# The local group's rotary halves laid 64 rows apart, swapped by two ScalarE copies; its k kept per kv head over 128 rows; another step order

## The chip, the cores and the metric

One core of a Trainium2 chip runs the kernel. The metric is the device time of one execution in microseconds (us); it is the median of three runs. The engines are TensorE (PE; its weight loads are PEld), VectorE (DVE), ScalarE (ACT), GpSimd (POOL) and SyncE (SP, which issues DMAs).

## The reference

Two layers over 512 tokens of width 1024, all in float32. Each layer normalises, projects, runs two attention groups, projects back, and runs an MLP:

```python
for l in range(DEPTH):                                   # DEPTH = 2
    h = rmsnorm(x, attn_norm[l])
    proj = jnp.einsum('bsd,de->bse', h, w_in[l])         # 2304 columns
    sb_q, sb_k, sb_v, sw_q, sw_k, sw_v = jnp.split(proj, splits, axis=-1)
    sb_o = stick_breaking_attention(sb_q, sb_k, sb_v)    # 8 heads of 64, causal, no softmax
    sw_q = rope(sw_q, positions)                         # 8 query heads of 64
    sw_k = rope(sw_k, positions)                         # 2 kv heads of 64
    sw_o = sliding_window_sink_attention(sw_q, sw_k, sw_v, sinks[l])   # window 128
    mix = concatenate([rmsnorm(sb_o, sb_norm[l]), rmsnorm(sw_o, swa_norm[l])])
    x = x + mix @ w_out[l]
    h = rmsnorm(x, mlp_norm[l])
    x = x + square(relu(h @ w_up[l])) @ w_down[l]        # 4096 wide
# rope: out = [x1 * cos - x2 * sin, x2 * cos + x1 * sin], x1 and x2 the two halves (32 each) of a head
```

## The kernel before

Activations are kept transposed: rows are features, 512 columns are tokens. Each float32 operand of the large products is split into a high part (rounded to fp32r) and a low part (the rest), and a product is three matmuls: high by high, high by low, low by high (L405 to L407). For the weights ACT makes the high part (step CH, L604) and POOL the low part (step CL, L804), and SP loads the next pack after it (L366).

The input projection makes 18 tiles of 128 rows. Tile n is made by the steps T (first four chunks of the contraction, 12 matmuls) and U (last four, 12 more) in bank n mod 2 of the PSUM tensor D. So tile n + 2 can start only when tile n is out of its bank. The way out depends on the kind of tile:

- q and k of the stick-breaking group: TE (DVE multiplies by the norm's factor, L989), TH (ACT writes the high part, L679 or L682), TL (DVE writes the low part, L1004 or L1008; then the bank counts as drained, L1011). For k of this group TH and TL are two instructions each, one for each head, with the other head's rows set to zero by a column of head_rows.
- v tiles: TE into kf, VT (PE transposes), VH and VL (ACT and DVE split).
- q and k of the local group (swq 0 to 3 and swk, the rotary tiles): RE (ACT copies the tile to kf, L689; SP then issues four DMAs of 32 rows that lay the halves exchanged into the one tensor turned, L381), RM (POOL multiplies turned by sin_r, L854), RS (DVE multiplies the tile in its bank by cos_r, L993), RA (DVE adds the two, L998), TH, TL. sin_r and cos_r have the norm's factor in them and are made once in each layer by the step RR (L973, L975). The next RE waits until the RA before it is done with turned.

The rotary tiles are tiles 3, 4, 5, 9 and 10 of the first layer and 1, 2, 3, 9 and 10 of the second. Tile 5 of the first layer and tile 2 of the second are k.

The local attention works in 8 steps n (two groups of heads by four blocks of 128 queries): WS (PE: 4 matmuls that lay the band mask, L482, and 12 of scores, L487, over 64 rows, as the two kv heads lie in rows 0 to 63 and 64 to 127), WM, WE, WR, WN (softmax), WT (PE transposes), WH, WL, WA (PE: probabilities by v, L511), WO, WD, SQ and SA (squares for the norm). The stick-breaking attention works head by head: BS (PE scores, L525, L527), BE (ACT: three functions, L703 to L707), BP (DVE, L1021), BH (ACT, L710), BL (DVE, L1025), BX (PE: suffix sums, L537), XE and XH (ACT, L714, L719), XL (POOL, L849), BA (PE, L550), BO, BD. BS of the next head waits for XE of the one before, as all heads share the PSUM tensor Z.

The norm's factor of the input (rms_a) comes from PE sums of squares (steps NP and NA, L417) and a chain NAD, NAE, NAF on DVE and ACT. AG0 to AG11 (DVE) make the rotary angles and SN (ACT, with two table loads) their sine and cosine; both belong to the first layer. OS is the output projection of the local part, OE adds it to x.

The order of all steps is one written list for each layer (ORDER_0, ORDER_1). Every engine walks the list and takes the steps that are its own, in the order of the list; semaphores do the rest. After the lists come the output projection of the stick-breaking part and the MLP, as loops.

## Time and profile before

| | |
|---|---|
| median of three runs | 1242.49 us (1240.52 to 1242.96) |
| the profiled execution, its own time | 1243.44 us |
| its span, first to last instruction | 1241.6 us |
| mean granted TensorE clock | 0.982 of full |
| busy: PE, DVE, ACT, POOL | 95%, 43%, 44%, 46% of the span |

The profile's times count from the first instruction of the span. The first layer's attention stage, with its two projections, runs from 11 us to about 268 us, its MLP to 623 us, the second layer's attention stage from there to about 870 us. The share of busy time is a mean over all stages; "idle before" tells how long an engine stood before an instruction, and the name behind the arrow what it waited for.

### The profile page before, as it was taken

How to read it: one execution, taken by the hardware profiler on the slowest of the kernel's cores; microseconds unless marked ns; L12 is line 12 of the kernel's file. 1: busy time of each engine (PE TensorE's matmuls, PEld its weight loads, DVE VectorE, ACT ScalarE, POOL GpSimd, SP SyncE). 2: the span in 40 equal slices, each digit the busy share in tenths (PEclk: the TensorE clock that was granted, in tenths of full speed). 3: DMA queues.
4: the chain of work that ended last, by engine and by line, in shares of the span. 5: the costliest groups of instructions: out<-in, count | busy, mean ns of one | idle time of the engine just before them, and what ended most of it. 6: DMA issues, size and time to landing. Idle time of an engine off the chain costs nothing.

```text
span 1241.6 us, 15277 instructions
## 1 busy us (share of the span) xinstructions
...
## 2 busy tenths in 40 slices
...
GB/s 179 77 86 51 45 42 35 68 48 105 114 90 102 102 84 101 101 84 101 85 85 77 60 68 48 48 25 60 102 102 102 88 105 96 93 105 89 100 69 68
DMA packets 30773, 102.20 MB, mean 82 GB/s; under 512 B 4224, under 2 KB 4224, under 8 KB 30720
## 3 DMA queue, kind: packets, MB, share of 16 engines
...
## 4 chain that ended last, share of the span: by engine, by line
PE 84%; DVE 6%; ACT 4%; issue 2%; POOL 1%; DMA 1%; DVEq 1%; ACTq 0%; SPq 0%; POOLq 0%
PE D L405 24%; PE D L407 24%; PE D L406 24%; PE Z L537 4%; PE Z L525 2%; PE O L550 1%; PE W L487 1%; DVE xm L910 1%; PE O L511 1%; PE W L497 1%; PE W L482 1%; PE W L417 1%; DMA x<-in_x 1%; DVE stage L1025 1%; POOL turned L854 1%
## 5 line engine op out<-in xcount | busy, mean ns | idle before, releaser
L804 POOL TENSOR_TENSOR w<-raw,w 128x1024 fp32r<-128x1024 f32 x178 | 432.7, 2433 | 412.7 <-ACT w L604 404.1
L604 ACT ACTIVATE w<-raw 128x1024 fp32r<-128x1024 f32 x177 | 186.0, 1052 | 212.1 <-PE D L407 201.0
L405 PE MATMUL D<-stage,w 128*128 128x512 f32 x576 | 225.4, 391 | 0.0
L407 PE MATMUL D<-stage,w 128*128 128x512 f32 x576 | 224.2, 389 | 0.0
L406 PE MATMUL D<-stage,w 128*128 128x512 f32 x576 | 224.1, 389 | 0.0
L405 PE MATMUL D<-xm,w 128*128 128x512 f32 x512 | 200.7, 392 | 5.1 <-POOL w L804 2.7
L406 PE MATMUL D<-xm,w 128*128 128x512 f32 x512 | 199.3, 389 | 0.0
L407 PE MATMUL D<-xm,w 128*128 128x512 f32 x512 | 199.2, 389 | 0.0
L405 PE MATMUL D<-xa,w 128*128 128x512 f32 x352 | 143.7, 408 | 23.1 <-DVE xa L910 11.3
L1108 DVE TENSOR_TENSOR kf<-o 128x512 f32<-128x512 f32 x64 | 64.3, 1004 | 189.4 <-ACT o L774 189.3
L1122 DVE TENSOR_TENSOR D<-D,probs 128x512 f32<-128x512 f32 x64 | 44.8, 699 | 229.4 <-PE D L407 229.4
L407 PE MATMUL D<-xa,w 128*128 128x512 f32 x352 | 139.5, 396 | 0.0
L406 PE MATMUL D<-xa,w 128*128 128x512 f32 x352 | 139.4, 396 | 0.0
L405 PEld LDWEIGHTS D<-stage,w 128*128 128x128 f32 x576 | 108.3, 188 | 22.7 <-issue 0.5
L406 PEld LDWEIGHTS D<-stage,w 128*128 128x128 f32 x576 | 108.3, 188 | 22.6 <-issue 0.5
L407 PEld LDWEIGHTS D<-stage,w 128*128 128x128 f32 x576 | 108.1, 188 | 22.6
L405 PEld LDWEIGHTS D<-xm,w 128*128 128x128 f32 x512 | 96.1, 188 | 27.8 <-DVE xm L910 4.1
L406 PEld LDWEIGHTS D<-xm,w 128*128 128x128 f32 x512 | 96.1, 188 | 20.1 <-issue 0.5
L407 PEld LDWEIGHTS D<-xm,w 128*128 128x128 f32 x512 | 96.1, 188 | 20.1
L405 PEld LDWEIGHTS D<-xa,w 128*128 128x128 f32 x352 | 67.4, 191 | 40.2 <-issue 14.9
L774 ACT ACTIVATE o<-D 128x512 f32<-128x512 f32 x64 | 38.1, 595 | 136.9 <-PE D L407 136.9
L407 PEld LDWEIGHTS D<-xa,w 128*128 128x128 f32 x352 | 67.4, 191 | 14.8
...
## 6 DMA issues: line engine op xcount, KB each, us to landing
...
inv_freq<-in_inv_freq SPq DMA_DIRECT2D x1, 0.5 KB, 4.5
sinks<-in_sinks SPq DMA_DIRECT2D x1, 8.0 KB, 7.0
```

The costliest lines, as they stand in the source:

```text
L405: pe.matmul(bank, w[:, slot, 0, k], rhs[:, 0, c], start=start, stop=False)
L406: pe.matmul(bank, w[:, slot, 0, k], rhs[:, 1, c], start=False, stop=False)
L407: mm = pe.matmul(bank, w[:, slot, 1, k], rhs[:, 0, c], start=False, stop=stop)
L417: return pe.matmul(W[:, 0, :], minus_one[:, :].bitcast(F32), squares, start=start, stop=stop)
L482: pe.matmul(dst[g], ident_r[:, :], band[:, at0:], start=True, stop=False)
L525: pe.matmul(dst, k[:, kl, j * P:(j + 1) * P], q[:, ql, j * P:T], start=f == 0 and j != 3, stop=False, skip_group_check=True)
L537: mm = pe.matmul(Z[:, at0:Z_AT[j] + Z_LEN[j]], (minus_tri if jj == j else minus_one)[:, :], sp[:, f, Z_AT[jj]:Z_AT[jj] + Z_LEN[jj]], start ...
L604: act.activation(w[:, slot_of(at_layer), 0], raw[:, p % 2], ACT.Identity).then_inc(w_hi, 1)
L774: act.activation(relu[c % 2], D[:, (MLP_TILE + c) % 2], ACT.Relu).then_inc(mlp_relu, 1)
L804: pool.tensor_tensor(w[:, slot, 1], raw[:, p % 2], w[:, slot, 0].bitcast(F32), ALU.subtract).then_inc(w_ready, 1)
L1108: dve.tensor_tensor(kf[:, c % 2], relu[c % 2], relu[c % 2], ALU.mult).then_inc(mlp_sq, 1)
L1122: dve.tensor_tensor(D[:, tile % 2], D[:, tile % 2], rms2, ALU.mult)
```

## The change

The columns of w_in for the local group's q and k are permuted on the host, so that a rotary tile has the first halves of its two heads in rows 0 to 63 and the second halves in rows 64 to 127; the frequencies of rows 0 to 63 are negative. A rotary tile now goes out of its bank so: TE (DVE, the norm's factor, in place), RE (two ACT copies of 64 rows each, to the other half of kf), RM (POOL: kf by sin, in place), RS (DVE: the bank by cos), RA (DVE: adds kf), TH, TL. The four DMAs, the tensor turned, sin_r, cos_r and the step RR are gone, and RE no longer waits for the RA of the rotary tile before. A row half now holds rows of both kv heads, so k is kept once for each kv head over all 128 rows with the other head's rows zero (group_rows): its TH and TL are two instructions each, and the 12 score matmuls of WS go over 128 rows. Squares of the local output (SQ) go to rms_w. Both step lists are new. Cut to its core:

```diff
@@ -107,40 +107,40 @@
 
 
 ORDER_0 = """
-AG0 T0 NP0 CH3 NA0 AG1 NAD0 U0 NAE0 NAF0 TE0 CL3 AG2 TH0 T1 TL0 U1 CH4 CL4 AG3 AG4 T2 TE1 CH5 TH1 TL1 CL5 U2
-T3 AG5 TE2 VT2 VH2 CH6 AG6 AG7 AG8 AG9 AG10 VL2 U3 RE3 AG11 CL6 RM3 T4 U4 SN0 RR0 BS0 CH7 RS3 RA3 RE4 TH3 TL3
-RS4 RM4 BE0 T5 RA4 TH4 CH8 U5 BP0 TL4 T6 RE5 BH0 RM5 U6 BL0 RS5 RA5 CL7 TE6 TH5 TL5 VT6 WS0 VH6 VL6 WM0 WE0
...
-BH4 WD5 BL4 CL17 WT6 TE15 BO3 TE14 BX4 WH6 SQ5 WL6 SA4 WS7 BD3 VT15 XE4 TH14 WM7 TL14 WA6 CH18 VH15 CL18 WO6
-WE7 BS5 VL15 WR7 T16 XH4 U16 WD6 BE5 WN7 WT7 T17 BP5 XL4 WH7 SA5 WL7 BH5 BL5 WA7 U17 BX5 CH19 TE16 TH16 WO7
-SQ6 WD7 TL16 SQ7 CL19 SA6 CH20 SA7 NW0 NWD0 XE5 NWE0 NWF0 TE17 MN0 BS6 VT17 BE6 CL20 CH21 MN1 GH0 BP6 MN2 BH6
...
-OS1 OE0 XL6 BO5 BP7 BH7 BD5 CH22 GH2 BL7 OS2 BA6 OE1 BX7 BO6 CL21 GL2 XE7 OE2 OS3 OE3 XH7 CL22 OS4 CH23 BD6
-OE4 XL7 BA7 BO7 OS5 BD7 OE5 OS6 CH24 NS0 CL23 CL24 GH3 NSD0 NSE0 GL3 OS7 OE6 NSF0 OE7
+T0 U0 NP0 CH3 AG0 AG1 NA0 AG2 NAD0 NAE0 T1 U1 NAF0 TE0 TH0 AG3 TL0 AG4 T2 TE1 U2 CH4 AG5 CL3 TH1 TL1 T3 TE2
+VT2 AG6 VH2 AG7 AG8 AG9 AG10 U3 CH5 VL2 AG11 SN0 TE3 RE3 CL4 CH6 T4 U4 RS3 RM3 CL5 RA3 TH3 TE4 TL3 BS0 RE4 T5
+RM4 RS4 RA4 TH4 U5 CL6 BE0 TL4 TE5 BP0 RE5 BH0 T6 RS5 RM5 BL0 CH7 RA5 U6 TH5 BX0 CH8 CL7 TE6 TL5 VT6 XE0 WS0
+WM0 WE0 WR0 CL8 VH6 XH0 VL6 BS1 CH9 T7 WN0 WT0 WH0 WL0 XL0 T8 WS1 BE1 CL9 CH10 WM1 WE1 BP1 WA0 U7 WO0 WR1 WN1
+TE7 U8 WT1 TH7 CL10 WH1 WD0 BH1 TL7 WL1 TE8 SQ0 T9 TH8 WS2 CH11 U9 BL1 WA1 WM2 SA0 TE9 WE2 WO1 WR2 BX1 RE9 XE1
+WN2 BA0 WD1 RM9 BO0 WT2 RS9 TL8 WH2 BS2 CH12 RA9 WL2 WS3 WM3 BD0 BE2 T10 WA2 CL11 CH13 TH9 CL12 BP2 WE3 U10
...
+SQ4 WD5 BH4 BL4 U15 BA3 WN6 WT6 TH14 WH6 BX4 XE4 TE15 VT15 BO3 WL6 TL14 WS7 VH15 SA3 WM7 SQ5 BS5 T16 WA6 VL15
+XH4 U16 WE7 BD3 BE5 WR7 SA4 WN7 WO6 BP5 WT7 CH18 T17 TE16 WH7 WD6 WL7 BH5 WA7 XL4 CL18 SA5 CH19 SQ6 BL5 WO7
+U17 WD7 SA6 SQ7 TH16 GH0 BX5 SA7 NW0 XE5 GL0 TL16 NWD0 NWE0 NWF0 GH1 BS6 BE6 MN0 CL19 GL1 TE17 VT17 VH17 BP6
+MN1 BH6 BA4 MN2 BL6 XH5 BO4 MH0 BD4 MH1 BX6 MH2 XE6 MN3 ML0 XL5 BA5 MH3 BS7 BO5 ML1 XH6 BE7 ML2 XL6 CH20 ML3
+CL20 OS0 VL17 BD5 BP7 OS1 BH7 OE0 BA6 GH2 OE1 CH21 BO6 OS2 BL7 CH22 BX7 OS3 CL21 XE7 XH7 BD6 OE2 CH23 CL22 OE3
...
 """
 ORDER_1 = """
-T0 CH3 NA0 T1 U0 NAD0 NAE0 CL3 U1 NAF0 RR0 TE0 TH0 RE1 TL0 RS1 CH4 CH5 RM1 T2 RA1 U2 TH1 TL1 RE2 CL4 RS2 T3 U3
-RM2 RA2 RE3 TH2 TL2 RS3 RM3 RA3 CH6 CL5 T4 TH3 CL6 TL3 U4 WS0 TE4 T5 WM0 WE0 VT4 VH4 CH7 U5 VL4 TE5 WR0 TH5
-WN0 T6 TL5 WT0 WH0 CH8 BS0 U6 WL0 BE0 CL7 BP0 WS1 T7 BH0 TE6 WM1 BL0 U7 CH9 VT6 WE1 WR1 BX0 TE7 VH6 XE0 VL6
...
+T0 CH3 NA0 NAD0 CL3 U0 T1 NAE0 NAF0 TE0 TH0 TL0 U1 T2 TE1 CH4 RE1 RS1 U2 RM1 CH5 RA1 CL4 TH1 TL1 TE2 RE2 RM2
+RS2 CL5 RA2 T3 TH2 TL2 CH6 U3 TE3 CL6 RE3 T4 U4 RS3 CH7 RM3 RA3 TH3 TL3 TE4 WS0 WM0 WE0 T5 VT4 VH4 WR0 U5 WN0
+CL7 VL4 WT0 T6 WH0 TE5 TH5 U6 TL5 TE6 BS0 WL0 WS1 CH8 VT6 CL8 T7 U7 BE0 WM1 CH9 VH6 BP0 VL6 CL9 BH0 BL0 WE1
+TE7 WR1 TH7 CH10 T8 BX0 WA0 WN1 WT1 XE0 WH1 WL1 WO0 BS1 WS2 TL7 U8 BE1 WD0 WM2 WA1 BP1 WE2 WR2 SQ0 BH1 T9 CH11
...
 """
...
         w = sb("w", [P, SPLIT_SLOTS, 2, KC, P], F32R)
         work = sb("work", [P, 2, Z_ALL])
-        ksw = sb("ksw", [P, 2, T], F32R)
+        ksw = sb("ksw", [P, KV_HEADS, 2, T], F32R)
         qsw = sb("qsw", [P, 2, 2, T], F32R)
         vsw = sb("vsw", [P, NB, KV_HEADS, 2 * DH], F32R)
         probs = sb("probs", [P, 4, 2 * P])
@@ -262,9 +262,8 @@
...
         kf = sb("kf", [P, 2, T])
-        turned = sb("turned", [P, T])
         head_rows = sb("head_rows", [P, 2])
-        sin_r = sb("sin_r", [P, T])
+        group_rows = sb("group_rows", [P, KV_HEADS])
...
         count, turns, theta = Z3[:, 0, :], cos[:, :], sin[:, :]
-        cos_r = rms_w[:, :]
-        sq_w = turned[:, :].rearrange("p (s i t) -> p s i t", s=2, i=2)
+        sq_w = rms_w[:, :].rearrange("p (s i t) -> p s i t", s=2, i=2)
...
-                    elif step == "RE":
-                        r = plan.re_use[step, n]
-                        sp_.wait_ge(kf_moved, l * ROPE_TILES + r + 1)
-                        for a in range(4):
-                            b = a ^ 1
-                            sp_.dma_start(turned[b * 32:b * 32 + 32, :], kf[a * 32:a * 32 + 32, n % 2]
-                                          ).then_inc(turned_in, 16)
...
-                                    half = slice(g * DH, (g + 1) * DH)
-                                    mm = pe.matmul(dst[g], qsw[half, i, ql, b * P:(b + 1) * P],
-                                                   ksw[half, kl, k0 * P:(b + 1) * P], start=False, stop=f == 2)
+                                    mm = pe.matmul(dst[g], qsw[:, i, ql, b * P:(b + 1) * P],
+                                                   ksw[:, g, kl, k0 * P:(b + 1) * P], start=False, stop=f == 2)
...
+                        elif kind == "swk":
+                            for g in range(KV_HEADS):
+                                last = act.activation(ksw[:, g, 0], D[:, n % 2], ACT.Identity, scale=group_rows[:, g:g + 1])
...
                     elif step == "RE":
-                        act.wait_ge(tile_done, l * DENSE + n + 1 + CREDIT)
-                        if plan.re_use[step, n]:
-                            before = next(x for x in plan.re_use if plan.re_use[x] == plan.re_use[step, n] - 1)[1]
-                            act.wait_ge(scaled, l * IN_TILES + plan.scaled["RA", before] + 1)
-                        act.activation(kf[:, n % 2], D[:, n % 2], ACT.Identity,
-                                       scale=SCALE if plan.tiles[n][0] == "swq" else 1.0).then_inc(kf_moved, 1)
+                        act.wait_ge(scaled, l * SCALES + plan.scaled["TE", n] + 1)
+                        for a in range(2):
+                            last = act.activation(kf[head(1 - a), n % 2], D[head(a), n % 2], ACT.Identity)
+                        last.then_inc(kf_moved, 1)
...
                     elif step == "SQ":
                         pair, b = divmod(n, NB)
                         act.wait_ge(swa_o, l * SWA_STEPS + n + 1)
-                        act.wait_ge(scaled, l * IN_TILES + plan.scaled["RA", plan.rope_last] + 1)
...
                     elif step == "RM":
-                        pool.wait_ge(turned_in, (l * ROPE_TILES + plan.re_use["RE", n] + 1) * 64)
-                        pool.wait_ge(sin_ready, l + 1)
-                        pool.tensor_tensor(turned[:, :], turned[:, :], sin_r[:, :], ALU.mult).then_inc(turned_sin, 1)
+                        pool.wait_ge(kf_moved, l * ROPE_TILES + plan.re_use["RE", n] + 1)
+                        pool.wait_ge(trig, 1)
+                        pool.tensor_tensor(kf[:, n % 2], kf[:, n % 2], sin[:, :], ALU.mult).then_inc(turned_sin, 1)
...
-                    elif step == "RR":
-                        dve.wait_ge(trig, 1)
-                        dve.scalar_tensor_tensor(sin_r[:, :], sin[:, :], -1.0, rms_a[:, :], ALU.mult, ALU.mult
-                                                 ).then_inc(sin_ready, 1)
-                        dve.tensor_tensor(cos_r, cos[:, :], rms_a[:, :], ALU.mult)
-                        dve.drain()
...
@@ -986,16 +979,16 @@
                         kind, j = plan.tiles[n]
                         dst = kf[:, n % 2] if kind in ("sbv", "swv") else D[:, n % 2]
                         dve.wait_ge(tile_done, l * DENSE + n + 1 + CREDIT)
-                        dve.scalar_tensor_tensor(dst, D[:, n % 2], SCALE if kind == "sbq" else 1.0, rms_a[:, :],
+                        dve.scalar_tensor_tensor(dst, D[:, n % 2], SCALE if kind in ("sbq", "swq") else 1.0, rms_a[:, :],
                                                  ALU.mult, ALU.mult).then_inc(scaled, 1)
                     elif step == "RS":
                         dve.wait_ge(kf_moved, l * ROPE_TILES + plan.re_use["RE", n] + 1)
-                        dve.scalar_tensor_tensor(D[:, n % 2], D[:, n % 2], SCALE if plan.tiles[n][0] == "swq" else 1.0, cos_r,
-                                                 ALU.mult, ALU.mult)
+                        dve.wait_ge(trig, 1)
+                        dve.tensor_tensor(D[:, n % 2], D[:, n % 2], cos[:, :], ALU.mult)
                         dve.drain()
                     elif step == "RA":
                         dve.wait_ge(turned_sin, l * ROPE_TILES + plan.re_use["RE", n] + 1)
-                        dve.tensor_tensor(D[:, n % 2], D[:, n % 2], turned[:, :], ALU.add).then_inc(scaled, 1)
+                        dve.tensor_tensor(D[:, n % 2], D[:, n % 2], kf[:, n % 2], ALU.add).then_inc(scaled, 1)
...
+                        elif kind == "swk":
+                            for g in range(KV_HEADS):
+                                last = dve.scalar_tensor_tensor(
+                                    ksw[:, g, 1], D[:, n % 2], group_rows[:, g:g + 1],
+                                    ksw[:, g, 0].bitcast(F32), ALU.mult, ALU.subtract)
...
-    in_columns[3 * SB_W:3 * SB_W + SWA_W] = 3 * SB_W + swa_rows
+    turn = np.arange(P).reshape(2, 2, DH // 2).transpose(1, 0, 2).reshape(-1)
+    in_columns[3 * SB_W:3 * SB_W + SWA_W] = 3 * SB_W + swa_rows.reshape(PAIRS, P)[:, turn].reshape(-1)
+    in_columns[3 * SB_W + SWA_W:3 * SB_W + SWA_W + P] = 3 * SB_W + SWA_W + turn
...
-    inv_freq[(np.arange(P) // half) % 2 == 1] *= -1
+    inv_freq[:DH] *= -1
...
```

## Rows read from the trace of the kernel before

**Rows 1.** Windows: stretch, then PE, PEld, DVE, ACT, POOL busy, clock, DMA

```profile
291.00:626.00 335.00, 335.00 (x1477) 277.12 (x1477) 103.20 (x136) 107.89 (x139) 156.55 (x68) 1.00 0.29 96
...
671.10:792.00 120.90, 120.45 (x716) 103.38 (x716) 64.98 (x100) 91.33 (x157) 62.18 (x34) 1.00 0.18 57
```

**Rows 2.** Waits of PE in 641:653 us, then in 50:66 us (sum, times, longest)

```profile
PE D L405 <- DVEq L1011: 4.9, 2, 2.6
...
PE D L405 <- DVEq L1011: 2.1, 2, 1.0
PE D L468 <- DVE kf L989: 0.8, 1, 0.8
```

**Rows 3.** Timeline, the rotary chain of tile 1, second layer (start, us, instruction)

```profile
636.38 0.60 ACT L689 ACTIVATE kf<-D 128x512 f32<-128x512 f32 x1 [1.11 <-PE D L407]
...
637.00 9.92 SPq L381 DMA_DIRECT2D turned<-kf  x8
...
640.87 1.29 POOL L854 TENSOR_TENSOR turned<-turned,sin_r 128x512 f32<-128x512 f32 x1 [10.92 <-DMA turned<-kf]
...
642.19 0.70 DVE L998 TENSOR_TENSOR D<-D,turned 128x512 f32<-128x512 f32 x1 [4.48 <-POOL turned L854]
```

**Rows 4.** Timeline of PE: where tiles and BX7 start late, and what follows

```profile
175.75 0.54 PE L405 MATMUL D<-xa,w 128*128 128x512 f32 x1 [1.87 <-DVEq L1011]
...
180.17 0.39 PE L405 MATMUL D<-xa,w 128*128 128x512 f32 x1
...
226.05 0.73 PE L537 MATMUL Z<-stage,minus_tri 128*128 128x512 f32 x2 [2.15 <-DVE stage L1025]
...
644.44 0.47 PE L405 MATMUL D<-xa,w 128*128 128x512 f32 x1 [2.56 <-DVEq L1011]
...
652.50 0.47 PE L405 MATMUL D<-xa,w 128*128 128x512 f32 x1 [2.34 <-DVEq L1011]
...
656.60 0.63 PE L405 MATMUL D<-xa,w 128*128 128x512 f32 x1
```

**Rows 5.** Groups of instructions by form (busy us, mean ns, idle before)

```profile
L989 DVE SCALAR_TENSOR_TENSOR D<-D,rms_a 128x512 f32<-128x512 f32 x16 | 11.1, 697 | 4.8 <-PE D L407 3.9
...
L724 ACT ACTIVATE other<-O 64x512 f32<-64x512 f32 x16 | 9.5, 593 | 11.8 <-PE O L550 11.6
...
L1025 DVE TENSOR_TENSOR stage<-work,stage 128x1280 fp32r<-128x1280 f32 x16 | 26.6, 1660 | 7.7 <-ACT stage L710 7.3 <-issue 0.2
```

**Rows 6.** Timeline of PE: a whole step WS1, and a step WA1

```profile
76.16 0.45 PE L482 MATMUL W<-band,ident_r 128*128 128x256 f32 x2
...
78.07 0.50 PE L405 MATMUL D<-xa,w 128*128 128x512 f32 x1
...
94.94 1.12 PE L511 MATMUL O<-pt,vsw 128*128 128x256 f32 x8
95.89 0.70 PE L537 MATMUL Z<-stage,minus_tri 128*128 128x512 f32 x2
```

**Rows 7.** Timeline of PE, first layer: NP0 begins, its wait, U0, T2

```profile
16.14 1.02 PE L417 MATMUL W<-acc,minus_one 128*128 128x512 f32 x2
...
18.84 1.13 PE L417 MATMUL W<-probs,minus_one 128*128 128x512 f32 x2 [1.68 <-DVE probs L943]
...
21.97 0.80 PE L405 MATMUL D<-xa,w 128*128 128x512 f32 x1
...
31.28 0.47 PE L405 MATMUL D<-xa,w 128*128 128x512 f32 x1 [0.56 <-DVEq L1011]
```

**Rows 8.** Timeline of DVE and POOL, first layer: before TL14, and around BL7

```profile
171.63 2.37 DVE L1055 SCALAR_TENSOR_TENSOR small<-small,neg_sink 128x4 f32<-128x4 f32 x1
...
174.16 1.40 DVE L1004 SCALAR_TENSOR_TENSOR xm<-D,head_rows,xm 128x512 fp32r<-128x512 f32 x2
...
222.41 3.58 DVE L1025 TENSOR_TENSOR stage<-work,stage 128x1280 fp32r<-128x1280 f32 x1 [0.21 <-issue]
...
222.27 2.38 POOL L804 TENSOR_TENSOR w<-raw,w 128x1024 fp32r<-128x1024 f32 x1 [3.08 <-ACT w L604]
```

More of the change, by code:

```diff
@@ L115 @@
-WR2 WN2 WD1 TL8 XH1 WT2 BO0 WH2 RS9 BD0 RM9 BS2 WL2 RA9 T10 WS3 U10 XL1 BE2 TH9 CH13 WM3 TL9 WE3 WA2 RE10 T11
-CL13 BP2 BA1 WR3 WN3 WT3 WO2 RM10 BH2 BO1 CH14 WH3 RS10 WD2 BL2 WL3 RA10 TH10 BD1 U11 SQ0 BX2 TL10 TE11 SA0
-WA3 T12 XE2 WS4 WO3 SQ1 WM4 SQ2 XH2 CH15 TH11 TL11 WE4 WR4 U12 BS3 WN4 WT4 WD3 BE3 TE12 WH4 SA1 XL2 BP3 T13
-VT12 WL4 U13 WS5 VH12 VL12 TE13 SQ3 WM5 WA4 BH3 BL3 TH13 CL14 TL13 WE5 T14 BX3 WO4 WR5 XE3 CH16 BA2 WN5 WT5
-BS4 CL15 WH5 XH3 BO2 WD4 T15 SA2 BE4 SQ4 CL16 WL5 WS6 WM6 BD2 CH17 WE6 BP4 U14 WA5 WO5 WR6 XL3 U15 BA3 SA3 WN6
@@ new lines @@
+XE3 TH13 WD4 U14 CH17 BO2 XH3 TL13 WH5 SA2 BS4 CL16 BE4 BD2 WL5 XL3 WS6 WM6 WA5 T15 WE6 TE14 BP4 WR6 CL17 WO5
+SQ4 WD5 BH4 BL4 U15 BA3 WN6 WT6 TH14 WH6 BX4 XE4 TE15 VT15 BO3 WL6 TL14 WS7 VH15 SA3 WM7 SQ5 BS5 T16 WA6 VL15
+XH4 U16 WE7 BD3 BE5 WR7 SA4 WN7 WO6 BP5 WT7 CH18 T17 TE16 WH7 WD6 WL7 BH5 WA7 XL4 CL18 SA5 CH19 SQ6 BL5 WO7
+U17 WD7 SA6 SQ7 TH16 GH0 BX5 SA7 NW0 XE5 GL0 TL16 NWD0 NWE0 NWF0 GH1 BS6 BE6 MN0 CL19 GL1 TE17 VT17 VH17 BP6
+MN1 BH6 BA4 MN2 BL6 XH5 BO4 MH0 BD4 MH1 BX6 MH2 XE6 MN3 ML0 XL5 BA5 MH3 BS7 BO5 ML1 XH6 BE7 ML2 XL6 CH20 ML3
```

54 lines of the change are left out of this document (30 added, 24 removed).

## The prediction

> **What bounds the kernel.** I read the windows first. In the MLP PE is busy 335.00 of 335 us, and from 671 to 792 us, the middle of the second layer's attention, 120.45 of 120.9 [rows 1]. So PE's own work sets the time, and another engine's work is worth something only where PE stands. I then read PE's waits by stretch and its timeline for the places. Those that touch this change are few. Ahead of T3 and T4 of the second layer PE stands 4.9 us, ahead of T5 and T6 of the first 2.1 us [rows 2], each time for a bank that a rotary tile leaves late. Elsewhere it stands 1.68 us inside NP0 [rows 7], 1.87 us ahead of T16 and 2.15 us ahead of BX7 in the first layer [rows 4]. After some of these the granted clock falls to its half level: T16 takes 180.17 - 175.75 = 4.42 us and T4 656.60 - 652.50 = 4.10 us [rows 4], where such a block takes some 2.8 (12 matmuls, 0.23 us apart).
>
> **The second layer's start.** Before, tile 1's chain is: copied at 636.38, four DMAs, POOL at 640.87, DVE's add at 642.19 [rows 3], then TH and TL, and T3 at 644.44 [rows 4]: 8.1 us. From the copy's end (636.98) to POOL's start are 3.9 us of DMA. The new chain is TE 0.70, two copies of 64 rows (0.59 each, L724, together 1.1 to 1.2), POOL 1.29, add 0.70, TH 0.60 (as the copy that it resembles), TL 0.70 (as the add) [rows 3, 5], and some 0.3 of hand-overs: 5.4 us. RS lies beside POOL's multiply as before. So bank 1 is free at 641.8, and PE, which came to it at 644.44 - 2.56 = 641.9, doesn't wait: 2.5 us gained. The wait that RE has for the add before it is gone, but it would not have been the last one.
>
> Tile 2 is k. It is done when T3 starts, 641.9. Its chain is 5.4 us, a second TH and TL (0.60 and 0.70) and a hand-over: 6.8, so T4 can start at 648.7. PE gets there at 641.9 + 5.7 = 647.6, waits 1.1, and is 652.50 - 648.7 = 3.8 ahead. Its longest idle stretch there is now 1.1 in place of 2.56 and 2.34, so I take the half-clock stretch in T4 (4.10 - 2.8 = 1.3) as gone: 5.1 us in all; I take 5.0. Tile 3 is done at 647.6; its TE waits behind TL2 until 648.7, and 5.4 later, at 654.1, it is out; WS0 comes at 648.7 + 5.7 = 654.4 and does not wait. RM1 and RM3 stand behind CL steps in POOL's queue, but those wait for splits that ACT makes earlier than now. Bounds: 3.7 if the clock still falls, 5.5 if T4 waits only 0.7.
>
> **The first layer's start.** U0 now stands ahead of NP0. PE fills the 1.68 us wait, but the sums start at 16.14 + 2.73 = 18.87, where the second of them could go on at 18.84 before [rows 7]; the first is now behind it (0.86), so the norm's factor comes 0.8 later. T2 waits for tile 0, and that for the factor: 31.28 + 0.8 = 32.1, with PE standing 3.8 us ahead of it rather than 0.56, as U0 and U1 are done by 28.3. That is a loss of 0.8, and 1.3 more if the clock falls there as it did in T16. Behind it the waits of T5 and T6, 2.1 us, and of VT6, 0.8 [rows 2], go: the same 2.7 us come off each rotary chain. SN0 now stands ahead of RE3, so tile 3's chain starts only after the tables (0.7 to 1.3 us past the old RE3's end) and takes back much of that for T5. BX0 and WS0 wait some 0.7 as BX0 is moved ahead of WS0. Sum: 2.1 + 0.8 - 0.8 - 0.7 = 1.4 without a fall of the clock, 0.1 with it. I take 0.8.
>
> **T16.** In DVE's list TL14 stood behind WM7 and BD3. WM7's 128x4 instruction took 2.37 us, TL14 came at 174.16 [rows 8], and PE stood 1.87 and then ran at half clock (4.42 - 2.8 = 1.6) [rows 4]. TL14 now stands ahead of WM7 and BD3, and TH14 ahead of XE4, so bank 0 is free before BS5 ends. The next gates, BX5 and NW0, hang on the same engines, which follow PE. Gain 3.2, between 1.9 (no clock) and 3.5.
>
> **BX7.** BL7 took 3.58 us, against 1.66 in its group [rows 5, 8]: it began 0.14 after a POOL split that took 2.38, and ended 1.3 after it. In the new list CH20 stands right behind BE7, so this split falls some 3 us earlier and reaches only the first 0.6 us of BL7. BL7 then ends near 223.4, when PE is still at BA6. The wait of 2.15 [rows 4] goes; I leave the clock behind it. Gain 2.1, between 0 (another split on the same spot) and 3.7 (with the clock).
>
> **Scores over 128 rows.** A step WS has 16 matmuls before and after. Before, it takes 78.07 - 76.16 = 1.91 us. WA has 8 matmuls of 256 columns over 128 rows, each with its own weight load, and takes 95.89 - 94.94 = 0.95, so 0.119 each [rows 6]. 16 x 0.119 = 1.90. So the wider rows cost nothing there, and I put 0.3 us for the four steps of 128 columns. Upper end: at 1.12 / 8 = 0.14 each the step takes 2.24, and 16 steps cost 5.3; lower end 0.
>
> A rule speaks against this edit. The Trainium skill, "TensorE: Matmul & The Clock Gate", Part 3 (Packing small matmuls), says that matmuls of few rows in distinct row groups run concurrently, starting within about 4 ns of each other. By it the 12 products now run as 6 pairs, the old step costs 10 slots, and the sum would be that of the rival below. The trace doesn't bear out a step of 10 slots.
>
> **The added work in the queues.** ACT gets 10 second copies and 2 second TH (7.1 us), DVE 10 TE and 2 second TL less 4 instructions of RR (about 5.6). POOL's work is the same, SP loses 40 DMAs and issues weights no later. The tiles of the two starts are in the chains above. In the middle are four tiles (9 and 10, twice). ACT has 29.6 us free of 120.9 there, DVE 56 [rows 1]; the rotary tiles have 10 us and more of PE work between U and the tile that wants their bank. If that cover is gone, the four cost 0.70 + 0.59 each, 5.2 us. New waits from a list in another order fall here too. I take 0.9.
>
> **The sum.** 5.0 + 0.8 + 3.2 + 2.1 - 0.3 - 0.9 = 9.9 us. The profiled execution took 1243.44 us for a span of 1241.6; it would take 1233.5, the span 1231.7. The median lies 0.95 below the profiled one's: 1242.5 - 9.9 = 1232.6.
>
> **Rivals.**
> *Given back in the tails.* The end of each layer's stage is a chain of heads through ACT and DVE. If T16 and BX7 only move their waits to BX6, 5.3 go: 1237.9. For it: BX7's gain hangs on half a microsecond between POOL and DVE. Against: T16's wait ends at a DVE queue, which is reordered. Chance 0.15.
> *Nothing stays.* The second layer's gain is also met by later waits: about 1242. Against it, PE stands 0.45 us in 120.9 behind it [rows 1]. Chance 0.06.
> *The pairs are lost.* If the score products pair up fully now, a WS step loses 6 slots of 0.119, 0.71 us, times 16: 11.4 in place of 0.3, and the time is 1243.7. Against it stands that the step takes 1.91 us and not 10 slots, 1.19 [rows 6]. Chance 0.04.
> *Slower: the heads fall behind.* ACT's list is filled up where a head's chain (BE, BH, XE) has to be ready when PE comes to BX. Each such miss costs its wait and then a half-clock block, as at T16: 1.87 + 1.6 = 3.5 us [rows 4]. Three such misses eat the gain; from 12.4 us, so with four among the heads that PE doesn't wait for now, the kernel is slower by over 0.2%: 1232.6 + 14 = 1246.6. For it: less PE work lies between BS4 and BX4 of the first layer than before (U14 has moved ahead of BS4). Against: ACT's 29.6 us of room. Chance 0.10.
>
> **How the numbers follow.** My forecast has 0.65. The range: best case 5.5 + 1.4 + 3.5 + 3.7 = 14.1 with nothing lost, so 1228.4, and other meetings of DVE and POOL can give a microsecond more: 1227. Its upper end takes in the rival in the tails and half of the unknown bounds: 1239.5. Left out are the last three rivals, 0.20. 0.2% is 2.5 us, about what a measurement can tell from no change. Faster by more than that (forecast and first rival): 0.80. Within: 0.10. Slower: 0.10.
>
> **What would show it.** T3 of the second layer without a wait and T4 with about 1.1; no half clock there; T2 of the first layer with a wait near 3.8; T16 right behind BS5; a WS step of about 1.9 us; BL7 near 2 us. I would be wrong if WS took 2.3 or more, if PE showed waits of over 1 us between 90 and 170 or in the second layer's middle, or if T2 started a long half-clock stretch.

## The result, and the profile after

The changed kernel takes 1223.74 us (1223.23 to 1226.46, 4 runs) against 1242.14 (1240.52 to 1242.96, 4 runs) for the kernel before: ratio 0.9858, 95% interval 0.984 to 0.9876. It is 18.4 us faster; 9.9 were forecast, and the time lies 3.3 us below the forecast range. The profiled execution of the changed kernel is the slowest of its four, 1226.46 us, span 1224.6, so the two traces differ by 17.0 us. The medians differ by 1.4 more. One execution of each kernel was profiled, so what the granted clock happened to do in that one is in every difference of the two traces.

PE does 5574 matmuls in both. So the time can be located by a *lead*: how much earlier than in the kernel before PE begins the same step, after the same PE work. The lead is 1.0 at tile 9 of the first layer, 4.6 behind T16, 8.0 behind BX7, 10.4 at the second layer's first matmul, 16.3 when its starting tiles are done, and 17.7 at the end of its list and at PE's last matmul. Over the whole span it is 17.0: the last 0.7 go in the output's stores, behind PE's work.

**The second layer's start.** PE's waits in 636 to 650 us, the stretch that answers to [rows 2]:

```profile
PE D L400 <- DVEq L1009: 1.2, 1, 1.2
```

The timeline of tile 1's chain, from TE to TL, with T3 on PE below it. It answers to [rows 3] and to T3 in [rows 4]; columns as there:

```profile
625.94 0.70 DVE L982 SCALAR_TENSOR_TENSOR D<-D,rms_a 128x512 f32<-128x512 f32 x1 [1.76 <-PE D L402]
...
627.95 1.29 POOL L853 TENSOR_TENSOR kf<-kf,sin 128x512 f32<-128x512 f32 x1 [8.43 <-ACT kf L684]
...
629.27 0.70 DVE L991 TENSOR_TENSOR D<-D,kf 128x512 f32<-128x512 f32 x1 [0.67 <-POOL kf L853]
630.63 0.69 DVE L1006 TENSOR_TENSOR qsw<-D,qsw 128x512 fp32r<-128x512 f32 x1 [0.66 <-ACT qsw L679]
...
631.52 0.47 PE L400 MATMUL D<-xa,w 128*128 128x512 f32 x1 [0.18 <-DVEq L1009]
```

The chain takes 631.32 - 625.94 = 5.4 us, and 5.6 to the start of T3, where it was 8.1. Tile 2, with its second TH and TL, goes from TE at 631.46 to the end of TL at 636.83 + 1.41 = 638.24: 6.8 us.

**The tail of the first layer.** Windows of the changed kernel around T2, T16, BX7 and the second layer's first tiles (columns as in [rows 1]):

```profile
31.53:35.55 4.02, 4.02 (x13) 3.18 (x13) 2.93 (x4) 0.60 (x1) 1.77 (x1) 0.68 0.31 89
171.72:175.00 3.28, 3.28 (x18) 2.60 (x18) 2.62 (x6) 3.21 (x11) 0.01 (x1) 1.00 0.00 0
219.65:222.50 2.85, 2.85 (x22) 2.75 (x21) 1.36 (x2) 1.06 (x1) 2.21 (x2) 1.00 0.30 108
631.50:644.00 12.50, 11.26 (x49) 8.95 (x50) 6.25 (x9) 6.25 (x9) 7.43 (x5) 1.00 0.36 126
```

and of the kernel before around T16, BX7 and T4 of the second layer, the blocks of [rows 4]:

```profile
175.75:180.17 4.42, 4.42 (x12) 3.50 (x13) 1.71 (x5) 4.22 (x7) 3.15 (x2) 0.61 0.22 84
226.05:230.50 4.45, 4.45 (x21) 4.36 (x22) 2.02 (x3) 0.00 (x0) 0.00 (x0) 0.63 0.28 107
652.50:656.60 4.10, 4.10 (x13) 3.19 (x14) 0.90 (x2) 0.03 (x1) 1.57 (x2) 0.67 0.21 51
```

The third number from the end is the granted clock. T16, BX7 and T4 each stood behind a wait of 1.9 to 2.3 us and ran mostly at the lower level (1.2 GHz); in the changed kernel T16 and BX7 wait for nothing, T4 waits 1.22, and all three run at the full 2.4 GHz. T2 of the first layer has the one new block at the lower level, behind a wait of 2.58 us.

Not each of these blocks comes whenever its wait does. The traces of the experiments below have the same waits again. BX7's of 2.1 us has a block at the lower level behind it in all five traces that have it. T16's of 1.9 us has one in two of six (before and `x_wide_scores`). `x_ch22` has the wait, 1.89 us, and then:

```profile
175.85:178.80 2.95, 2.95 (x13) 2.45 (x14) 1.71 (x5) 2.87 (x5) 1.68 (x1) 1.00 0.32 126
```

So 1.6 us of what the trace of before shows at T16 come in some executions and not in others. T2's wait of 2.58 us has a block at the lower level behind it in two of five traces (the changed kernel and `y_t16`).

**A place that was not forecast.** DVE and POOL of the kernel before, just past the end of the first layer's list, where NSF0 makes the norm's factor for the MLP in three operations (the timeline):

```profile
247.00 0.69 DVE L902 TENSOR_TENSOR rms_a<-rms_a,work 128x512 f32<-128x512 f32 x1
248.14 2.86 DVE L904 SCALAR_TENSOR_TENSOR rms_a<-rms_a,work 128x512 f32<-128x512 f32 x1 [0.44 <-issue]
...
248.08 2.37 POOL L804 TENSOR_TENSOR w<-raw,w 128x1024 fp32r<-128x1024 f32 x1 [3.95 <-ACT w L604]
...
251.91 0.47 PE L405 MATMUL D<-xa,w 128*128 128x512 f32 x1 [2.35 <-DVE x L1090]
```

(the last row is PE, at the second tile behind the list) and of the changed kernel:

```profile
239.79 0.69 DVE L903 SCALAR_TENSOR_TENSOR rms_a<-rms_a,work 128x512 f32<-128x512 f32 x1
...
240.12 2.63 POOL L798 TENSOR_TENSOR w<-raw,w 128x1024 fp32r<-128x1024 f32 x1 [3.96 <-ACT w L598]
```

Before, the third operation pauses 0.44 us, comes 0.06 after POOL's low part and takes 2.86; after, there is no pause, it comes 0.33 ahead of POOL and takes 0.69. OE7 stands behind NSF0 in DVE's order, and PE waits 2.35 us for OE7's bank before and not at all after. The lead rises by 2.45 there.

### The profile page after: what moved, and what is told of

Its sections match the earlier page's. It is cut to its first block, busy times and chain, and to the rows that moved or that the text cites. A ratio compares the mean times of both kernels' runs of the same rounds, so it can differ in the third digit from the quotient of the medians.

```text
span 1224.6 us, 15260 instructions
## 1 busy us (share of the span) xinstructions
PE 1173.8 (96%) x5574; PEld 980.7 (80%) x5574; DVE 543.0 (44%) x719; ACT 555.8 (45%) x805; POOL 572.9 (47%) x296
## 4 chain that ended last, share of the span: by engine, by line
PE 84%; DVE 5%; ACT 3%; issue 2%; POOL 2%; POOLq 1%; DVEq 1%; DMA 1%; SPq 0%; ACTq 0%
PE D L400 24%; PE D L401 24%; PE D L402 24%; PE Z L531 4%; PE Z L519 2%; PE W L481 2%; POOL w L798 2%; DVE xm L909 1%; PE O L544 1%; PE O L505 1%; PE W L491 1%; PE W L412 1%; POOLq L806 1%; PE W L477 1%; ACT work L709 1%
```

## Experiments

### The new lists without the copies, the copies without the new lists

`x_dma_new_list` is the kernel before with the new lists. RR is put back, the rotary tiles have no TE, and SQ0, SQ1, SA0 (and SA1) stand behind TH10, as squares go to turned there. All else is as before:

```diff
-ORDER_0, ORDER_1 of before
+ORDER_0, ORDER_1 of after, without TE of tiles 3, 4, 5, 9, 10 (second layer: 1, 2, 3, 9, 10)
+... SN0 RR0 ... TH10 SQ0 SQ1 SA0 ...      second layer: NAF0 RR0 ... TH10 SQ0 SQ1 SA0 ... TL10 SA1
```

> The kernel before (DMAs for the halves, sin_r and cos_r, 64-row scores) with the new step lists; TE of the rotary tiles left out, RR put back behind SN0 and NAF0, and SQ0, SQ1, SA0, SA1 put behind TH10, as squares and halves share a tensor. Theory A, the lists carry most of the gain: T16 (3.6 us), BX7 (3.8) and the stretch after the list of the first layer (2.4) are gained without the copies, about 9.8 us, so 1232 to 1234; the waits ahead of T3, T4 of the second layer and T5, T6 of the first stay. Theory B, the shorter rotary chain makes the room that the lists use: 1240 or more.

Measured: 1253.52 us (1252.24 to 1254.08) against 1241.55, ratio 1.0092 (1.0075 to 1.0109). PE's waits in 45 to 80 us, and in 640 to 670 us:

```profile
PE D L403 <- DVEq L1009: 4.1, 1, 4.1
PE Z L535 <- DVE stage L1023: 1.5, 1, 1.5
...
PE D L403 <- DVEq L1009: 5.5, 2, 3.0
PE W L480 <- DVE qsw L1006: 3.6, 1, 3.6
```

`x_copies_old_list` is the changed kernel with the old lists; each TE of a rotary tile stands right ahead of its RE, and TL0 of the second layer ahead of TE1:

```diff
-... VL2 AG11 SN0 TE3 RE3 ...              (first layer, after)
+... VL2 U3 TE3 RE3 AG11 CL6 RM3 T4 U4 SN0 BS0 ...
```

> The kernel after with the old step lists: RR left out, TE of a rotary tile right ahead of its RE (in the second layer TL0 is moved ahead of TE1). Theory A: T3 of the second layer gains its 2.5 us, but T4 gains only 1 in all, as the old list has RE3 ahead of TH2 on ScalarE and RE3 now waits for TE3 behind U3; the first layer's start gains 2 to 3 us; T16, BX7 and the stretch after the first list stay. In all 2 to 5 us: 1237 to 1240. Theory B (the chain carries the gain whatever the list): 1230 or less.

Measured: 1245.72 us (1244.57 to 1246.9), ratio 1.0037 (1.0024 to 1.005). PE's waits in the same stretches:

```profile
PE D L398 <- DVEq L1007: 2.2, 1, 2.2
PE W L475 <- DVE ksw L1000: 1.6, 1, 1.6
PE D L461 <- DVE kf L980: 1.3, 1, 1.3
...
PE D L398 <- DVEq L1007: 5.1, 2, 4.9
```

Each half alone, in the form tried here, makes the kernel slower, by 12.0 and by 4.2 us; together they take 18.4 off. (In the trace of `x_copies_old_list` the meeting at NSF0 is gone as well, which is worth 2.5 us; so the copies under the old lists lose more than 4.2 elsewhere.) The short chain gives its 2.5 us at T3 with the old list too, but there RE3 stands ahead of TH2 in ACT's queue and waits for its tile, so T4 waits 4.9. The new list, in turn, brings each tile's matmuls where the longer chain of DMAs can't follow. A sum of parts, each measured from the kernel before, would have given the wrong sign.

### Each layer's list by itself

`y_l0_old`: the changed kernel, the first layer's list as in `x_copies_old_list`:

```diff
-ORDER_0 of after
+ORDER_0 of x_copies_old_list
```

> The changed kernel with the first layer's list of the kernel before (each TE of a rotary tile right ahead of its RE) and the second layer's new list. If each layer's list works on its own, the first layer's part of the gain goes: its matmuls then lead those of before by about -0.2 us at the start of the second layer (as with both old lists) in place of +10.4, and the second layer still gains its 6 to 7, 1234.3 us. If the two lists need each other (carried states: splits ahead, the queue's order of packs), the second layer loses as well: 1238 or more. If the first layer's old list costs nothing, 1224.

Measured: 1237.84 us (1237.06 to 1240.32), 14.1 over the changed kernel. The lead over the kernel before is -1.5 at the second layer's first matmul (with 2.2, 1.6 and 1.3 us of the same waits at T5, WS0 and VT6), and rises to 6.4 by the end of the list: 7.9 us, where the changed kernel has 17.7 - 10.4 = 7.3. Some 1.4 of either is not the new list's (see the tail of the second layer below). So the second layer's gain is its own; the forecast of this run was 3.5 low, because the first layer with the old list is not a return to the kernel before but worse than it, as in `x_copies_old_list`. That the added work of DVE and ACT found no room made for it there is how I read this; it was not tested by itself.

### The two tail terms

`x_three`, the kernel before with three moves in the first layer's list:

```diff
-WL6 BD3 WM7 TL14       (DVE)
+WL6 BD3 TL14 WM7
-BH7 CH22 GH2           (ACT)
+BH7 GH2 CH22
-NSD0 GL3 OE6 NSF0      (DVE)
+OE6 NSD0 GL3 NSF0
```

> The kernel before with three steps of the first layer's list moved: TL14 ahead of WM7, CH22 behind GH2, OE6 ahead of NSD0. Theory A: the wait ahead of T16 goes with its half clock (3.5), BL7 no longer meets a POOL split so BX7 starts 2.1 us earlier and with full clock (3.7), and the last step of the norm's factor no longer meets the split that follows the list (2.4): 9.6 us, 1232.5. Rival: each freed wait comes back at the next gate (BX6, NW0, the first tiles of the next projection), 1239 or more.

Measured: 1237.75 us (1235.47 to 1240.0), ratio 0.9967 (0.9955 to 0.998). Three moves in an unchanged kernel give 3.8. The lead rises by 3.7 at T16, but 1.6 of it is the clock of the profiled execution of before: `x_ch22` and `x_pad`, in which T16 waits as before, gain 1.6 and 1.5 there too. A wait of 1.15 at WA7 takes back 1.4 of the rest, so the move of TL14 leaves 0.7. The lead rises by 3.7 at BX7. The move of OE6 gives nothing: NSF0's pause and its 2.86 us stay.

`x_ch22`, only the move of CH22:

```diff
-BD5 CH22 GH2 BL7
+BD5 GH2 CH22 BL7
```

> The kernel before with CH22 of the first layer behind GH2, nothing else. If BL7 and POOL's low part side by side are the whole of BX7's 2.15 us and of the half clock behind it, 3.7 us less: 1238.3 us. If only the wait goes and the half clock stays, 1239.9; if PE meets another wait behind it, 1242.

Measured: 1238.2 us (1236.91 to 1239.87) against 1242.35, ratio 0.9967 (0.9958 to 0.9977). DVE's BL7, POOL's low part, and the window of BX7:

```profile
220.30 1.49 DVE L1024 TENSOR_TENSOR stage<-work,stage 128x1280 fp32r<-128x1280 f32 x1 [0.21 <-issue]
...
221.90 2.39 POOL L803 TENSOR_TENSOR w<-raw,w 128x1024 fp32r<-128x1024 f32 x1 [4.31 <-ACT w L603]
...
221.84:224.70 2.86, 2.86 (x21) 2.77 (x21) 2.86 (x2) 0.60 (x1) 2.39 (x1) 1.00 0.02 6
```

Apart, BL7 takes 1.49 us, not 3.58 [rows 8], and BX7 runs at the full clock. The lead rises by 3.7 at BX7. One step moved by one place is worth 4.2 us by the medians (interval 2.9 to 5.2), wait and clock together, as much as the three moves of `x_three`.

`y_tail_undone` tried to take both back in the changed kernel:

```diff
-BO3 WL6 TL14 WS7 VH15 SA3 WM7 SQ5 ... WE7 BD3 BE5
+BO3 BD3 WL6 WS7 VH15 SA3 WM7 TL14 SQ5 ... WE7 BE5
-BH7 OE0 BA6 GH2 OE1 CH21
+BH7 OE0 BA6 CH21 GH2 OE1
```

> The changed kernel with three moves of the first layer's tail taken back: BD3 ahead of WL6, TL14 behind WM7, and one weight high part (CH21) between BH7 and GH2. If these orders are what gave 3.6 us at T16 and 3.8 at BX7, the time is 1231.0 us (3.7 with only one of them). If the new list's other differences gave the time, it stays at 1224.

Measured: 1232.57 us (1232.18 to 1233.81), 8.8 over the changed kernel, but not where it was expected. BD3 ahead of WL6 is an order of neither kernel and made WS7 wait 5.22 us. And BX7 kept all its gain: BL7 started 1 us ahead of CL21 and took 1.61. So in the changed kernel ACT's order is not all that keeps the two apart; DVE's, BD5 ahead of BP7, may do it as well.

`y_bl7_late` therefore put BD5 behind BP7 again, with CH21 moved as above:

```diff
-BD5 BP7 OS1 BH7 OE0 BA6 GH2 OE1 CH21
+BP7 BD5 OS1 BH7 OE0 BA6 CH21 GH2 OE1
```

> The changed kernel with BD5 of the first layer behind BP7, so that BL7 starts behind it, and the high part CH21 between BH7 and GH2. If BX7's 3.8 us came from BL7 no longer lying beside POOL's low part, the two now lie side by side again as in the kernel before (BL7 at 222.41, POOL at 222.27), BL7 takes about 3.6 us, BX7 waits some 2 us and half clock follows: 1227.5 us. If BL7 starts first and POOL's operation is the one that takes longer (as with CH21 alone moved, where BL7 kept 1.6 us), or if BX7's gain lies elsewhere, 1224.

Measured: 1232.53 us (1230.31 to 1232.69), 8.8 more. The meeting came, but at BD5, whose operations stretch beside POOL (DVE's timeline, then POOL's):

```profile
214.79 1.61 DVE L1033 TENSOR_TENSOR other<-o 128x512 f32<-128x512 f32 x1
216.49 2.72 DVE L1035 TENSOR_TENSOR acc<-acc,other 128x512 f32<-128x512 f32 x1
...
213.49 2.37 POOL L797 TENSOR_TENSOR w<-raw,w 128x1024 fp32r<-128x1024 f32 x1 [1.99 <-ACT w L597]
216.32 2.34 POOL L797 TENSOR_TENSOR w<-raw,w 128x1024 fp32r<-128x1024 f32 x1 [0.46 <-ACT w L597]
```

BD5 lets O go, so BA6 waited 5.38 us: some 3.0 of it is the stretch of these two operations, the rest that BD5 stands behind BP7, which waits for ACT. So a meeting costs PE a wait here too, but the instruction hit and the price (8.8, not 3.8) were both misjudged. No run brought the meeting back at BL7 of the changed kernel, so which of the two orders keeps it away there stays open.

`y_t16`, DVE's order in the tail exactly as before:

```diff
-WL6 TL14 WS7 VH15 SA3 WM7 SQ5 ... WE7 BD3 BE5
+WL6 BD3 WS7 VH15 SA3 WM7 TL14 SQ5 ... WE7 BE5
```

> The changed kernel with DVE's order in the first layer's tail as in the kernel before: WL6, BD3, WM7, TL14 (BD3 alone ahead of WL6 was not that order and made WS7 wait 5.22 us). If TL14 ahead of WM7 is what gave 3.6 us at T16, T16 waits some 2.4 us, half clock follows, and the time is 1227.4 us. If the tile's shorter chain has already made room for WM7, 1224.

Measured: 1230.14 us (1229.0 to 1230.24), 6.4 over the changed kernel. The first two rows are TL14 on DVE, behind BD3 and WM7, and T16:

```profile
172.94 1.40 DVE L996 SCALAR_TENSOR_TENSOR xm<-D,head_rows,xm 128x512 fp32r<-128x512 f32 x2
...
174.54 0.47 PE L399 MATMUL D<-xa,w 128*128 128x512 f32 x1 [2.92 <-DVEq L1008]
```

T16 waits 2.92 us, a block at the lower clock follows, and WA6 is 4.1 later. The delay is 5.0 at BS6, which waits 1.06 itself.

### The pause at NSF0

`x_pad` is the kernel before with 16 drains more on DVE, where it still waits for the positions:

```diff
+            for _ in range(16):
+                dve.drain()
             dve.wait_ge(positions_loaded, 32)
```

> The kernel before with 16 drains of DVE more, ahead of its first wait, where it is idle. If the 2.45 us at the third operation of NSF0 come from a pause of 0.44 us that sits at a place in DVE's instruction stream and not from the work around it, the pause moves away, the operation starts ahead of POOL's split and takes 0.7 us, not 2.86: 1239.7 us. If the pause belongs to the operation or to the work around it, 1242, with the pause and the 2.86 us as before.

Measured: 1239.64 us (1238.12 to 1239.79) against 1241.98, ratio 0.9976 (0.9966 to 0.9986). NSF0's third operation and POOL's low part:

```profile
246.29 0.69 DVE L904 SCALAR_TENSOR_TENSOR rms_a<-rms_a,work 128x512 f32<-128x512 f32 x1
...
246.59 2.67 POOL L804 TENSOR_TENSOR w<-raw,w 128x1024 fp32r<-128x1024 f32 x1 [3.95 <-ACT w L604]
```

Sixteen instructions that do nothing make the kernel 2.3 us faster. The pause was there in the kernel before, `x_three`, `x_ch22`, `x_wide_scores` and `x_dma_new_list`, whatever their lists; it is absent in all with the changed program. A pause of this kind in the MLP moved with the padding as well: before, it stands at x += D at 949.45 (0.43), DVE's record 596; in `x_pad` at record 588, 922.18 (0.42). The shorter pauses, of 0.21 us, did not move, and `x_pad` has one of 0.43 at 713.63 that the kernel before has not. That the place in DVE's program decides, and not the work around it, is what these traces agree with; what the engine does there is not shown.

`y_pad`, the same padding in the changed kernel:

> The changed kernel with the same 16 drains of DVE more, ahead of its first wait. If pauses of about 0.4 us sit at places in DVE's instruction stream, they move to other operations here too; where none falls on an operation that another waits for, 1223.7 as without them, and a meeting with POOL in a new place would cost up to 2.5 us (1226.2). If the drains themselves were what made the padded kernel before faster, 1221.3.

Measured: 1224.24 us (1223.87 to 1225.5), ratio to the kernel before 0.9847 (0.9827 to 0.9866), where the changed kernel has 0.9858: no gain that can be told from none. The drains are worth nothing by themselves.

### Scores over 128 rows

`x_wide_scores`, the kernel before with the score matmuls over all 128 rows of q and k as they lie (so the products of both kv heads are added):

```diff
-qsw[half, i, ql, b * P:(b + 1) * P], ksw[half, kl, k0 * P:(b + 1) * P]
+qsw[:, i, ql, b * P:(b + 1) * P], ksw[:, kl, k0 * P:(b + 1) * P]
```

> The kernel before, with the 12 score matmuls of a step WS over 128 rows instead of 64 (the low and high parts of q and k as they are, so the scores of both kv heads are summed; nothing else differs). By the row of WA (0.119 us a matmul) a step stays at 1.9 us and the time at 1242.1, up to 1.3 us more as the kernel after showed 30.57 us for its 16 steps against 29.34. If the pairs of 64-row matmuls were worth six slots, 0.71 us a step, it takes 1253.

Measured: 1242.03 us (1240.75 to 1243.66), ratio 1.0001 (0.9991 to 1.001). The 16 steps themselves take 30.3 us, from the start of each to the start of the next step, against 29.34: 1.0 more, within the interval.

`y_narrow`, the changed kernel with 64 rows:

```diff
-mm = pe.matmul(dst[g], qsw[:, i, ql, b * P:(b + 1) * P], ksw[:, g, kl, k0 * P:(b + 1) * P], ...
+mm = pe.matmul(dst[g], qsw[head(g), i, ql, b * P:(b + 1) * P], ksw[head(g), g, kl, k0 * P:(b + 1) * P], ...
```

> The changed kernel with each kv head's scores over 64 rows, as before (rows 0 to 63 for the first, 64 to 127 for the second; it leaves out half of each dot product, so its output is not the reference's). If the wider operands cost what the steps' rows say, 16 score steps get 1.2 to 2.4 us shorter in all and the time is 1221.3 to 1222.5 us. If the wide scores cost nothing, or if PE's activity with all rows pays for it in the clock, 1223.7 or more.

Measured: 1222.66 us (1221.35 to 1225.07), 1.1 less than the changed kernel, with overlapping runs. From the start of a WS step to the start of the next step the 16 take 30.57 us wide and 29.54 narrow, 0.06 each; but between the first WS and the last the narrow kernel's lead over the changed one rises by only 0.3 in the first layer (1.1 to 1.4) and by nothing in the second (3.9 and 3.9). Most of what its profiled run is ahead comes from the clock: T2 of the first layer, behind the same wait of 2.58 us, ran at full clock in this run:

```profile
32.02:34.87 2.85, 2.85 (x12) 2.34 (x13) 2.70 (x4) 0.60 (x1) 1.78 (x1) 1.00 0.09 11
```

against 0.68 in the changed kernel's profiled run (the first window above). The steps up to there are the same in both kernels. This is 1.2 of the 5.0 us between the two profiled spans; BX6 of the first layer, at the full clock here too, is 2.2 more.

### Versions that beat both

`x_np0_first`, the changed kernel with the old order of the first sums:

```diff
-T0 U0 NP0 CH3 AG0 AG1 NA0 AG2
+T0 NP0 CH3 AG0 AG1 NA0 U0 AG2
```

> The changed kernel with U0 of the first layer moved behind NP0 and NA0, as before. If the order of these steps is what makes T2 of the first layer wait (2.58 us at 31.53, then 1.2 us of half clock), the norm's factor comes up to 2.9 us sooner, the wait and the half clock go, and the time is 1220 us. Rival: the squares that NA0 adds come no sooner, or DVE's copies of the high and low parts hold U0 or T1 instead: 1223.5 to 1225.

Measured: 1221.69 us (1221.01 to 1223.01), ratio to the kernel before 0.9835 (0.9819 to 0.9851), 2.05 less than the changed kernel. NP0 and NA0 begin at 16.46 and 20.48, T2 waits little:

```profile
31.10 0.47 PE L399 MATMUL D<-xa,w 128*128 128x512 f32 x1 [0.55 <-DVEq L1008]
```

`z_both` adds U17 of the first layer behind BS6, with all that writes xa behind it:

```diff
-WO7 U17 WD7 SA6 SQ7 TH16 GH0 BX5 SA7 NW0 XE5 GL0 TL16 NWD0 NWE0 NWF0 GH1 BS6 BE6 MN0 CL19 GL1 TE17 ...
+WO7 WD7 SA6 SQ7 TH16 BX5 SA7 NW0 XE5 TL16 NWD0 NWE0 NWF0 BS6 U17 BE6 GH0 MN0 TE17 VT17 VH17 BP6 GL0 CL19 ...
```

> A version meant to beat both: the changed kernel with U0 of the first layer behind NP0 and NA0 (measured alone: 2.05 us) and U17 of the first layer behind BS6, so that head 6's chain starts 2.9 us sooner and U17 fills the time in which PE waits at VT17 (3.64 us) and BX6 (1.98 us); GH0, GH1, GL0, GL1 and CL19 go behind U17, as they write the tensor that it reads. If the chain of head 6 is what ends last there, 2.9 us and part of the half clock at BX6: 1218.5 us. If the moved copies or TE17 hold BL6 instead, 1221.5.

Measured: 1222.36 us (1221.5 to 1223.2), ratio to the kernel before 0.9831 (0.9811 to 0.9851). `x_np0_first` has 0.9835, so the two can't be told apart, and the move of U17 is worth nothing that these runs show. VT17's wait falls from 3.64 to 0.79, but BX6's rises:

```profile
197.65 1.22 PE L530 MATMUL Z<-stage,minus_tri 128*128 128x512 f32 x2 [3.54 <-DVE stage L1022]
...
197.65:202.83 5.18, 5.18 (x21) 4.99 (x21) 4.97 (x5) 2.22 (x4) 2.73 (x1) 0.50 0.00 0
```

Most of the idle time was moved, not removed. BX6 starts 1.1 earlier than in `x_np0_first`, the clock is at its lower level (1.2 GHz) for all of it, and it ends 1.2 later. That is one execution of each, and behind a wait of 1.4 us BX6 took 4.9 us in `y_pad`, at the lower level, and 3.0 in `y_narrow`, at the full one. Whether this fall of the clock belongs to the longer wait is not shown.

## Why the prediction was right in kind and wrong in size

| term | forecast | in the two traces | other runs |
|---|---|---|---|
| second layer's start | 5.0 | 5.9 | 7.9 for the layer (`y_l0_old`) |
| first layer's start | 0.8 | 1.0, with 1.2 lost to the clock at T2 | T2's order costs 2.05 of what was to be had |
| T16 | 3.2 | 3.6, of it 1.6 clock | 2.1 without the clock when added alone, 1.4 of it given back at WA7; 6.4 when taken back |
| BX7 | 2.1 | 3.8 | 4.2 by medians and 3.7 in the trace, added alone |
| wide scores | -0.3 | -1.2 over the 16 steps, within the other terms | -0.1 to -1.1 |
| added work, new waits in the middle | -0.9 | 0 | |
| NSF0 beside POOL | none | 2.45 | 2.3 (`x_pad`) |
| tail of the second layer | none | 1.4 | 1.6 to 1.7 in four kernels with the old list |
| VT17 and BX6 of the first layer, and the output's stores | none | -1.1 | |
| sum | 9.9 | 17.0 | 18.4 by medians |

What the forecast lacks, in the two traces, is NSF0 (2.45), BX7's clock (1.7), 0.9 of the second layer's start and the 0.9 given to the middle. The best case behind the range, 14.1 us, had BX7's clock in it; NSF0 is the largest part of what lies beyond. The rest of the difference between the traces is the clock of the one execution of each, where the table names it; what the clock does between the medians was not measured.

*The second layer's start.* Right step by step: chains of 5.4 and 6.8 us as worked out, T3 without a wait of weight (0.18), T4 with 1.22 (forecast 1.1), no lower clock. Of the missing 0.9, 0.47 is a wait of BS0 in the kernel before, which I had not listed, and some 0.35 the rest of T4's block at the lower clock, which runs on into U4.

*The first layer's start.* The sum came out near, 1.0 for 0.8, but by luck in part: with a fall of the clock at T2 the forecast had 0.1. The fall came in this execution (1.2 us) and not in others, and made up for losses that did not come. T2 came at 31.53, not 32.1, and U1 ended at 28.95, not 28.3, so the wait was 2.58 and not 3.8; T5, T6, VT6, BX0 and WS0 wait for nothing.

*T16.* Right in place: T16 waits for nothing right behind BS5. The size, 3.6 for 3.2, holds between these two traces only. The forecast took the block at the lower clock behind T16 as belonging to the wait, and four of six traces with that wait don't have it.

*BX7.* The failed step is "I leave the clock behind it", and with it 2.1 in place of the 3.7 that stood as the bound. BX7's wait takes its block at the lower clock with it: with the wait of 2.15 gone, the granted clock over BX7 is 1.00, in `x_ch22` as in the changed kernel. I had counted the clock as gone at T16 and T4 and left it at BX7 without a row that sets BX7 apart. That BL7 and POOL's operation must not lie beside each other was the right mechanism: BL7 starts at 217.46, POOL's operation of 215.29 ends 0.25 later, and BL7 takes 1.60.

*The list of places.* The second failed step is in the first part of the prediction: "Those that touch this change are few." NSF0's 2.86 us stood in the trace of before, 2.2 us over its like, and PE waited for it; I took it as outside the change, as no step of it moved. But a changed program of DVE moves its pauses, and a pause decides who is first, DVE or POOL. The tail of the second layer is not the change's: BX6 waits 7.1 us before and after, and from its start to OS5 it is 29.9 us in the profiled execution of before and 28.6 in that of after, but 28.3 in `x_wide_scores`, `x_ch22`, `x_pad` and `x_three` and 28.9 in `x_copies_old_list`, which have the old list there. The clock around BX6 stayed at its lower level for longer in the one execution of before (granted clock 0.54 over 811 to 822 us, and 0.71 over the same stretch of `x_wide_scores`).

*The middle.* The 0.9 was not lost. In the second layer BL2 meets POOL's XL1 (both start at 707.46; BL2 takes 4.30, BX2 waits 1.26), which is a new wait as feared, but waits of 0.35 at WT4 and 0.55 at WA7 are gone, and the lead is 16.3 at BX6 as it was at T9.

*The rivals.* Given back in the tails: BX6 of the first layer waits 1.98, less than before (3.21), so no; but `x_three` shows this in part (1.4 us back at WA7), and `z_both` moves most of VT17's wait to BX6. Nothing stays: the second layer's attention stage has three waits of 1 us and more (T4, BX2, BX6), and the lead keeps to the end. The heads fall behind: nowhere in the changed kernel, but both half-changes are slower, by 12.0 and 4.2 us. The largest waits in their traces are for the banks of T3, T4 and T5 and for WS0, not for the heads' chains, so it is the rival's outcome and only in small part (BX0, BX2) its mechanism. The pairs are lost: `x_wide_scores` prices the wide rows in the kernel before at 0.1 us with an upper end of 1.2 (0.1%), not 11.4. The term itself was taken too low: 0.3, where the 16 steps got 1.0 (`x_wide_scores`) and 1.2 us longer. The Trainium skill, "TensorE: Matmul & The Clock Gate", Part 3 (Packing small matmuls), would have few-row matmuls in distinct row groups run side by side; these steps don't show it, at 1.83 us narrow and 1.91 wide on the mean.

*DVE beside POOL.* In [rows 8] BL7 starts 0.14 us after a POOL operation of 2.38 and ends at 225.99, 1.34 after POOL's end at 224.65: it gets almost all of its own 1.5 us only once POOL is done. NSF0's third operation, 0.06 behind POOL's, ends 0.55 after it, again about its own 0.69. Where DVE comes first (BL7 in `y_tail_undone`, NSF0 in the changed kernel) it keeps its time or nearly so, and POOL takes 2.6 to 2.9 in place of 2.4.

Not all of DVE's operations are held so. It depends on where their inputs lie. In the trace of before 18 operations of DVE of 128x512 with both inputs in SBUF begin while POOL has one of over 1 us with more than 0.3 us left: they take 1.37 to 2.86 us and end 0.55 after POOL's, all 18. Of the same shape, 60 with an input in a PSUM bank begin so, and take 0.68 to 0.70 as ever. In the changed kernel, the additions into x beside POOL (DVE, then POOL):

```profile
216.03 1.28 DVE L1088 TENSOR_TENSOR x<-D,x 128x512 f32<-128x512 f32 x2
...
215.29 2.42 POOL L798 TENSOR_TENSOR w<-raw,w 128x1024 fp32r<-128x1024 f32 x1 [2.20 <-ACT w L598]
```

The Trainium skill, "SBUF — State Buffer", section "SBUF: two separate sides", states this as a lock on the port pair that DVE and GpSimd share: a DVE operation with two SBUF inputs and a GpSimd operation that reads SBUF exclude each other, and the first to start holds the pair for its whole instruction. These rows agree. So the price of a meeting depends on who starts first: at NSF0, 0.06 us behind POOL costs 2.2 us.
